# One score product per pair of blocks in stick-breaking attention, and VectorE adding each key's own logarithm

## The reference

```python
log_beta = jax.nn.log_sigmoid(z)
log_stay = jnp.where(mask, log_beta - z, 0.0)          # mask: key_pos < q_pos
log_w = log_beta + lax.cumsum(log_stay, axis=3, reverse=True) - log_stay
w = jnp.where(mask, jnp.exp(log_w), 0.0)
out = einsum('bhqs,bhsd->bhqd', w, v)
```

## Time and profile before

| | us |
|---|---|
| median of 3 runs | 3321.93 (3318.65 to 3331.39) |
| the profiled execution, its own time | 3318.72 |
| its span | 3316.9 |
| PE busy | 3078.7 |
| DVE busy | 2420.3 |
| ACT busy | 1340.9 |
| mean granted TensorE clock | 0.969 |

### The profile page before, as it was taken

One profiled execution on the slowest core, in us unless ns is written; L12 is line 12 of the kernel. 1 busy time (PEld: TensorE's weight loads), 2 busy tenths in 40 slices (PEclk: granted clock), 3 DMA queues, 4 the chain that ended last, 5 costly groups with the idle time before them and its releaser, 6 DMA issues. The chain is left out here.

```text
span 3316.9 us, 45880 instructions
## 1 busy us (share of the span) xinstructions
PE 3078.7 (93%) x16440; PEld 2049.9 (62%) x16440; DVE 2420.3 (73%) x5311; ACT 1340.9 (40%) x3417; POOL 1326.1 (40%) x1040
## 2 busy tenths in 40 slices
PE   7999899889999999988699999998899999999887
PEld 2466488656666666655344565787666666666553
DVE  5874459988889878777721253499888888878777
ACT  3232122786555555400111153226866565555000
POOL 0000000655556767766300000005456656767664
PEclk9999999999999999999899989999999999999999
DMA  8510261989999999999812101518799999999998
GB/s 302 181 51 26 95 228 65 347 291 364 374 371 376 409 409 409 409 408 409 332 57 82 49 22 38 195 67 310 276 359 376 384 353 409 409 409 409 409 409 351
DMA packets 282682, 931.22 MB, mean 281 GB/s; under 512 B 31804, under 2 KB 32460, under 8 KB 281944
## 3 DMA queue, kind: packets, MB, share of 16 engines
q0 software_dynamic: 147840, 536.96, 41.6%
q1 hardware_dynamic: 134616, 391.34, 31.3%
HBM read 921.87 MB, written 6.32 MB: 280 GB/s over the span
## 5 line engine op out<-in xcount | busy, mean ns | idle before, releaser
L753 PE MATMUL psum<-hT,mod 128*128 128x256 f32 x4096 | 969.8, 392 | 64.0 <-ACT big L1211 38.6
L753 PEld LDWEIGHTS psum<-hT,mod 128*128 128x128 f32 x4096 | 782.2, 195 | 189.7 <-issue 86.7
L1221 ACT ACTIVATE levels<-key_numbers,hT 128x128 bf16<-128x128 f32 x1792 | 566.7, 389 | 138.0 <-PE psum L789 137.5
L1871 DVE SCALAR_TENSOR_TENSOR tmp<-w,small,tmp 128x1024 f32<-128x1024 f32 x339 | 435.7, 1285 | 82.3 <-DMA w<-in_peer_v,tmp 37.8
L2046 POOL DMA_INDIRECT w<-in_peer_u,tmp x172 | 236.4, 1374 | 584.2 <-DVEq L1702 447.3
L1851 DVE CUSTOM_DVE_ANT_0 w<-w,hn 128x1024 f32<-128x1024 f32 x342 | 408.7, 1224 | 73.5 <-DMA w<-in_peer_down,tmp 36.2
L2046 POOL DMA_INDIRECT big<-in_peer_down,tmp x86 | 117.5, 1366 | 720.0 <-DVEq L1702 633.7
L763 PE MATMUL psum<-rows,big 128*128 128x512 f32 x768 | 344.2, 592 | 3.3 <-DVE big L1804 3.3
L789 PEld LDWEIGHTS psum<-x,levels 128*128 128x128 bf16 x6144 | 225.7, 101 | 164.8 <-issue 100.9
L1224 ACT ACTIVATE levels<-levels 128x512 bf16<-128x512 bf16 x448 | 282.2, 630 | 14.2
L789 PE MATMUL psum<-x,levels 128*128 128x32 bf16 x6144 | 236.9, 196 | 50.5 <-DVE levels L1792 25.7
(11 more groups left out here) (328 smaller groups left out, 4179.7 us busy)
## 6 DMA issues: line engine op xcount, KB each, us to landing
mod<-in_uT SPq DMA_DIRECT2D x256, 512.0 KB, 6.8
rows<-in_peer_v SPq DMA_DIRECT2D x64, 512.0 KB, 6.8
rows<-in_peer_up SPq DMA_DIRECT2D x64, 512.0 KB, 6.8
w<-in_w_in SPq DMA_DIRECT2D x14, 2048.0 KB, 8.5
srow<-in_peer_v SPq DMA_DIRECT2D x32, 512.0 KB, 6.9
tmp<-in_peer_v SPq DMA_DIRECT2D x32, 512.0 KB, 6.8
srow<-in_peer_up SPq DMA_DIRECT2D x32, 512.0 KB, 6.8
tmp<-in_peer_up SPq DMA_DIRECT2D x32, 512.0 KB, 6.8
```

Source lines behind the costliest of these rows:

```text
L753: last = nc.tensor.matmul(ps[4 + e % 2][:, 0:ND], ub[e % UV][:, k, :], hT[:, k, ND:SEQ], start=k == 0, stop=k == KC - 1)
L1221: last = nc.scalar.activation(hits[n % HITS][:, j * P:(j + 1) * P], keyno, ACT.Abs, bias=nibT[:, n * BATCH + j:n * BATCH + j + 1])
L1871: last = stt(y, row, c8[g % 2][:, b:b + 1], y, ALU.mult, ALU.add)
```

## The change

The first constant matrix becomes the strict triangle, so that a tile's sum holds only later keys. TensorE no longer forms the score a second time: it sums the `stay` tiles alone into bank 6 or 7, the own block first and the later blocks after it. VectorE, after the softplus, makes a second pass over the same PSUM score and `ab` in place: min(z, 0) minus the logarithm, which is the key's own log_beta. For tile m it then waits for `ar_done`, adds the sum in PSUM to that buffer, writes the result to `st1` and raises a new semaphore, `w_added`. ScalarE waits for `w_added` of tile m in place of `ar_done` and raises `st1` in place. The `ab` buffers become four. The mask of the weights on VectorE moves one iteration later (m = n - 3), its loop has one more iteration, and `rstd` and `gated` move two iterations later. TensorE's wait before a sum becomes `w_added`, and the wait for the values of two heads before moves from ScalarE to VectorE.

```diff
--- before.py
+++ after.py
@@ -68,7 +68,7 @@
 
         "c_reset": np.broadcast_to((np.arange(SEQ) % CHUNK != 0).astype(np.float32), (P, SEQ)).copy(),
 
-        "c_sticks": np.stack([-(j >= i).astype(np.float32), -np.ones((P, P), np.float32),
+        "c_sticks": np.stack([-(j > i).astype(np.float32), -np.ones((P, P), np.float32),
                               (j < i).astype(np.float32)], 1).reshape(P, 3 * P),
 
         "c_decay": decay.astype(np.float32),
@@ -334,7 +334,7 @@
         rt = [part(tmp, 2 * n, 2) for n in range(2)]
         sq = part(tmp, 4, 2)
         t3 = part(tmp, 6, 2)
-        ab = [part(tmp, 2 * n, 2) for n in range(LOOK + 1)]
+        ab = [part(tmp, 2 * n, 2) for n in range(LOOK + 2)]
         z_bank = [ps[1], ps[4], ps[5]]
         stay = [part(big, 8 * n, 8).rearrange("p (j n) -> p j n", j=NT) for n in range(2)]
         wide_sq = part(tmp, 10, 2)
@@ -427,6 +427,7 @@
         sp_ready = sem("stays_ready")
         ar_done = sem("stick_logs_summed")
         w_exp = sem("weights_raised")
+        w_added = sem("own_logs_added")
         wt_ready = sem("weights_ready")
         picks_ready = sem("dense_picks_ready")
         picks_turned = sem("dense_picks_turned")
@@ -975,13 +976,12 @@
                 if m >= 0:
                     h, j = m // NT, NT - 1 - m % NT
                     if m >= 2:
-                        pe.wait_ge(w_exp, m - 1)
+                        pe.wait_ge(w_added, m - 1)
                     bank = ps[6 + m % 2]
-                    score(h, j, bank, True, False)
                     pe.wait_ge(sp_ready, m + 1)
-                    for i in range(NT - 1, j - 1, -1):
+                    for i in range(j, NT):
                         last = nc.tensor.matmul(bank[:, (i - j) * P:SEQ - j * P], sticks[:, 0 if i == j else 1, :],
-                                                stay[h % 2][:, i, i * P:SEQ], start=False, stop=i == j)
+                                                stay[h % 2][:, i, i * P:SEQ], start=i == j, stop=i == NT - 1)
                     last.then_inc(ar_done, 1)
                     if h and j == NT - 2:
                         stick_values(h - 1)
@@ -1332,10 +1332,10 @@
             for n in range(STICKS + LOOK):
                 if n < STICKS:
                     wd = SEQ - (NT - 1 - n % NT) * P
-                    z, l = z_bank[n % (LOOK + 1)][:, 0:wd], ab[n % (LOOK + 1)][:, 0:wd]
+                    z, l = z_bank[n % (LOOK + 1)][:, 0:wd], ab[n % (LOOK + 2)][:, 0:wd]
                     act.wait_ge(z_done, STICKS + n + 1)
-                    if n > LOOK:
-                        act.wait_ge(z_used, n - LOOK)
+                    if n >= LOOK + 2:
+                        act.wait_ge(w_added, n - LOOK - 1)
                     step(nc.scalar.activation(l, z, ACT.Abs))
                     step(nc.scalar.activation(l, l, ACT.Exp, scale=-1.0))
                     nc.scalar.activation(l, l, ACT.Ln, bias=1.0).then_inc(ln_ready, 1)
@@ -1349,10 +1349,9 @@
                 m = n - LOOK
                 if m >= 0:
                     h, j = m // NT, NT - 1 - m % NT
-                    act.wait_ge(ar_done, m + 1)
-                    if j == NT - 1:
-                        act.wait_ge(pv_done, 8 + 8 + h - 1)
-                    nc.scalar.activation(st1[h % 2][:, j, j * P:SEQ], ps[6 + m % 2][:, 0:SEQ - j * P], ACT.Exp).then_inc(w_exp, 1)
+                    act.wait_ge(w_added, m + 1)
+                    w = st1[h % 2][:, j, j * P:SEQ]
+                    nc.scalar.activation(w, w, ACT.Exp).then_inc(w_exp, 1)
                     if j == 0 and h >= 1:
                         head_out(h - 1, 64, 512, 8 + 8 + h, stick_sq[(h - 1) % 2], 8 + 4 + h - 2 if h >= 3 else 0)
             head_out(7, 64, 512, 8 + 8 + 8, stick_sq[1], 8 + 4 + 6)
@@ -1974,7 +1973,7 @@
                 nc.vector.tensor_reduce(ss_sticks.rearrange("p (t h) -> p t h", t=NT)[:, :, h],
                                         stick_sq[h % 2].rearrange("p (t n) -> p t n", t=NT), AX_X, ALU.add).then_inc(heads_summed, 1)
 
-            for n in range(STICKS + LOOK):
+            for n in range(STICKS + LOOK + 1):
                 if n in (1, 4, 7, 10):
                     dve.wait_ge(pv_used, 8 + 8)
                     centred(n // 3)
@@ -1982,11 +1981,11 @@
                     seen.next(ss_done)
                     t = n // 3 - 1
                     nc.vector.tensor_reduce(ss[:, 8 * t:8 * t + 8], by_head(wide_sq, 8, 64)[0], AX_X, ALU.add).then_inc(heads_summed, 1)
-                if n == 13:
+                if n == 15:
                     dve.wait_ge(heads_summed, 8 + NT)
                     rstd(8 * NT, 64)
-                if n in (14, 16, 18, 20):
-                    gated(n // 2 - 7)
+                if n in (16, 18, 20, 22):
+                    gated(n // 2 - 8)
                 if n < STICKS:
                     h, j = n // NT, NT - 1 - n % NT
                     wd = SEQ - j * P
@@ -1997,11 +1996,21 @@
                         else:
                             dve.wait_ge(z_done, STICKS + 1)
                     sv_ = stay[h % 2][:, j, j * P:SEQ]
-                    stt(sv_, z_bank[n % (LOOK + 1)][:, 0:wd], 0.0, ab[n % (LOOK + 1)][:, 0:wd], ALU.max, ALU.add).then_inc(z_used, 1)
+                    z, l = z_bank[n % (LOOK + 1)][:, 0:wd], ab[n % (LOOK + 2)][:, 0:wd]
+                    stt(sv_, z, 0.0, l, ALU.max, ALU.add)
+                    stt(l, z, 0.0, l, ALU.min, ALU.subtract).then_inc(z_used, 1)
                     dve.wait_ge(z_used, n + 1)
                     sv_ = stay[h % 2][:, j, j * P:(j + 1) * P]
                     tt(sv_, sv_, sticks[:, 2, :], ALU.mult).then_inc(sp_ready, 1)
                 m = n - LOOK
+                if 0 <= m < STICKS:
+                    h, j = m // NT, NT - 1 - m % NT
+                    wd = SEQ - j * P
+                    dve.wait_ge(ar_done, m + 1)
+                    if j == NT - 1:
+                        dve.wait_ge(pv_done, 8 + 8 + h - 1)
+                    tt(st1[h % 2][:, j, j * P:SEQ], ps[6 + m % 2][:, 0:wd], ab[m % (LOOK + 2)][:, 0:wd], ALU.add).then_inc(w_added, 1)
+                m = n - LOOK - 1
                 if m >= 0:
                     h, j = m // NT, NT - 1 - m % NT
                     dve.wait_ge(w_exp, m + 1)
```

## The result

| | before | changed |
|---|---|---|
| median of the runs, us | 3326.14 (4 runs, 3318.65 to 3331.39) | 3352.25 (4 runs, 3351.72 to 3355.45) |
| ratio of the two | | 1.0086, 95% interval 1.0072 to 1.0101 |
| granted clock, whole span | 0.969 | 0.96 |

The account below looks back on a forecast made before the run. TensorE was taken to pace the steady heads before, and turns between ScalarE and VectorE after. 16 us from the turns and 9 from the clock made 25 us on 3318.72, 3344, median 3347 us; range 3330 to 3369 us.

Parts of the forecast that it names:

- The likeliest case: Whole kernel: turns of ScalarE and VectorE plus a partly halved TensorE clock, 25 us longer, median 3347 us, chance 0.52.
- TensorE sets the pace before, and the stage is the path: Stage before the change: PE paces steady heads at 11.75 us; a microsecond in the 106.4 us stage is one of the kernel.
- The removal saves 2.2 us a head: TensorE's score products: half go, saving 2.2 us a head, so PE needs about 9.5 us a head.
- VectorE's second pass and addition: 3.9 us a head: VectorE's added work in the stage: 3.9 us a head, 31 us in all, making its 52 busy us some 83.
- ScalarE and VectorE take turns, 14.7 us a head: Steady heads: the two engines wait for each other with little overlap, 14.7 us a head against 11.75.
- The root costs 3.05 us: Head 3: the root's two table loads of 1.28 us and the hand-over lie on the path, making it 17.75 us.
- At full clock +16 us: Whole stage at full clock: heads and tail sum to 122.6 us, 16 us more than 106.4.
- The clock adds 9 us: TensorE in the stage: half of the heads at half clock, 2.2 us each, 9 us more.
- the prediction's own signs: Stage profile: large waits for Ln, the addition and PE's `sp_ready` or addition; steady heads 14.5 to 17 us; clock below 0.89.
- Rival 1: Stage: turns of ScalarE and VectorE but TensorE at full clock, +16 us, 3338 us; chance 0.22.
- Rivals 3 and 4: Stage: rival 3, ACT and DVE overlap more, 3322 us, chance 0.09; rival 4, PE remains the bound, 3304 us, chance 0.06.
- Rival 2: Stage: clock stays at 1.2 GHz mostly and PE's 19 us a head set it, +46 us, 3368 us; chance 0.11.

Follow-up runs that it names:

- the fillers: Changed kernel plus three unused 512-column TensorE products a head, after the sums of its first two tiles; stage 141.6 us, ratio 1.0061 to the kernel before.
- the run with ScalarE freed: Changed kernel, but ScalarE raises the sum straight from PSUM, not waiting for VectorE's addition; own logarithm left out of the weights; stage 133.9 us, ratio 1.0027.
- the version with the later exponential: Changed kernel with ScalarE's exponential and the mask of the weights one iteration later, values after the third tile's sums; stage 151.3 us, ratio 1.0056.
- the kernel with the addition first: Changed kernel with VectorE's addition of tile n - 2 ahead of everything else in iteration n; stage 144.0 us, ratio 1.0086 to the kernel before.

## Why the prediction was right

It gave 3347 us and a ratio of about 1.0075; 3352.25 and 1.0086 came. It used the median of three runs, 3321.93, which a fourth moved to 3326.14, so that its 25 us stand against 26.1 between the medians and 28.5 in the stage. The likeliest case is the one that happened. Two errors, in TensorE's need and in the mask of the weights, left the total alone only because the turns were longer; that was luck. Point by point:

- *TensorE sets the pace before, and the stage is the path.* Shown: with half the scores gone and nothing else changed the stage is 10.1 us shorter and the kernel 0.31% faster.
- *The removal saves 2.2 us a head.* Mis-sized: 1.53 us. I halved the time of a group whose members run partly side by side. Scores of neighbouring heads lie on different halves of the partitions (`heads[h % 2]` in `score`), and the trace shows such a pair running side by side: before, the 128-column score of one head and the 384-column score of the head before it take 0.85 us together, from the first product to the next group, and in the run without the second score the 384-column one alone takes 0.83:

```profile
1979.29 0.92 PE L960 MATMUL psum<-big 64*128 64x128 f32 x4
1980.14 1.57 PE L983 MATMUL psum<-big,levels 128*128 128x128 f32 x6
...
2000.29 0.91 PE L960 MATMUL psum<-big 64*128 64x384 f32 x2
...
2001.12 0.49 PE L982 MATMUL psum<-big,levels 128*128 128x128 f32 x2
```

The first two lines are of before, the others of the run. In the same way the 256- and 512-column pair took 1.05 us. The 384- and 128-column scores of one head, which lie on the same half, took 1.06, longer than the 384 alone by the time of the 128. Over the four tiles of a head it is 4.44 us before, of which half is my 2.2, and 2.92 in the run. TensorE's need is 10.2 us a head, not 9.5. At full clock both are shorter than a turn.
- *VectorE's second pass and addition: 3.9 us a head.* Right: 15.4 + 15.6 = 31.0 us for eight heads, 3.88 each.
- *ScalarE and VectorE take turns, 14.7 us a head.* One turn of the changed kernel in its timeline (start us, length us):

```profile
2014.55 0.58 ACT L1339 ACTIVATE tmp<-psum 128x512 f32<-128x512 f32 x1
...
2015.16 0.63 ACT L1340 ACTIVATE tmp<-tmp 128x512 f32<-128x512 f32 x1
2015.82 0.63 ACT L1341 ACTIVATE tmp<-tmp 128x512 f32<-128x512 f32 x1
2016.48 0.69 DVE L2000 SCALAR_TENSOR_TENSOR big<-psum,tmp 128x512 f32<-128x512 f32 x1 [1.98 <-ACT tmp L1341]
2017.09 0.68 DVE L2001 SCALAR_TENSOR_TENSOR tmp<-psum,tmp 128x512 f32<-128x512 f32 x1
2017.80 0.29 DVE L2004 TENSOR_TENSOR big<-big,levels 128x128 f32<-128x128 f32 x1
2018.01 0.42 DVE L2012 TENSOR_TENSOR hT<-psum,tmp 128x256 f32<-128x256 f32 x1
...
2018.17 0.79 PE L961 MATMUL psum<-big 64*128 64x128 f32 x2
...
2018.46 0.42 ACT L1354 ACTIVATE hT<-hT 128x256 f32<-128x256 f32 x1 [2.02 <-DVE hT L2012]
...
2032.88 0.79 PE L961 MATMUL psum<-big 64*128 64x128 f32 x2
```

ScalarE's three steps run to 2016.45; VectorE's first pass starts at 2016.48 and its addition, last of four, at 2018.01; ScalarE's exponential starts at 2018.46 with 2.02 us of idle time ahead of it; VectorE's first pass had 1.98 us of it. From the first product of this head to that of the next it is 14.71 us (2018.17 to 2032.88), at full clock for most of it. It is the shortest of the later heads here; with the fillers four heads took 14.2 to 14.8. That the wait for the addition costs time is shown by the run with ScalarE freed.
- *The root costs 3.05 us.* From the first table load to the exponential it took 3.4 us; its head took 19.3 us against the 17.75 laid out:

```profile
1978.56 1.28 ACT L1025 ACT_TABLE_LOAD   x1
...
1980.44 0.23 ACT L1025 ACTIVATE small<-small 128x32 f32<-128x32 f32 x1 [0.60 <-DVE small L1391]
1980.69 1.28 ACT L1348 ACT_TABLE_LOAD   x1
...
1981.98 0.31 ACT L1354 ACTIVATE hT<-hT 128x128 f32<-128x128 f32 x1
```

- *At full clock +16 us.* The changed kernel with TensorE kept busy, the nearest to that case, is at +15.4 us, with fillers and 35 us at half clock in it (31 before). No run has the turns alone at a clock of 1.00.
- *The clock adds 9 us.* Right in kind, too small: 13.1 us came back with the fillers. The share was near: I had half of the heads at half clock, and 85 of the 154.7 us were. The price was too low: I took 2.2 us for a head at half clock, and the 50 us less of it with the fillers gave back 13.1, by which a head of 15 us at half clock costs some 4 (an estimate). The heads from first read to first read took 11.0, 16.0, 18.1, 19.3, 14.8, 17.7 and 15.6 us against 11.3, 15.6, 14.7, 17.75, 15.3, 15.3 and 14.7 laid out for full clock: 7.8 us over. From there to the last products with the values it was 22.6 us against 18.0, another 4.6. Together 12.4, near the 13.1. The Trainium skill ("TensorE: Matmul & The Clock Gate", "A second HAM failure mode") tells of a kernel in which short and frequent idle times of TensorE between groups of matmuls made its clock go up and down. The trace agrees: it falls nine times in the stage, with no wait of PE for the mask longer than 3.0 us in the waits view.

Turn and clock overlap: 20.8 and 13.1 us one by one, 28.1 together (154.7 to 126.6). By the ratios it is 15 and 4 us one by one, and 22 together. Part of the overlap is that the run with ScalarE freed also lost 26 us of half clock; how far a turn hides a slow matmul was not measured by itself.

What the prediction left out: it took the later mask of the weights as free. In the changed kernel PE waits 16.4 us for it ahead of the values, seven times, and in the version with the later exponential it was the next bound. By the prediction's own signs PE should have waited long for the masked softplus (`sp_ready`) or for the addition; it shows 2.5 us for the first, and 7.2 us of its weight loads for the second. Steady heads were to take 14.5 to 17 us: two of them took 18.1 and 17.7.

Rival 1 fell with the clock of 0.72. Rivals 3 and 4 fell with the turns. Rival 2 had the clock low for most of the stage, and 85 of the 154.7 us were at 1.2 GHz, but TensorE at that clock did not set the pace throughout: it came back in every head.

That the clock falls because TensorE has too little work between its waits is shown by the three fillers a head that held it; which of the gaps decides was not taken apart.

## What to carry to other kernels

Moving work onto an engine that has room by busy time is only half a sum: write down, for each engine, what stands behind each wait, and look for a loop between two engines A and B in which A, after its step n, waits for B's finishing step n - 2, which in B's order stands behind B's step n, which waits for A's step n. Break it by a lag of one iteration more (that alone gained 3.4 us of the 28.5 here), and then look again at everything that hung on the old lag (here the values and the next score behind them). When TensorE is relieved of work and has gaps, count its remaining work at half clock too. And a product that is taken away is worth what it costs beside its neighbours: two that run side by side cost little more than the longer one.

## What the runs showed of the hardware that I had not expected

TensorE with 24 products added was through the same stage sooner than without (141.6 against 154.7 us in the traced executions), with the granted clock at 0.87 in place of 0.72; the kernel's times show only 1.0061 against 1.0073, with overlapping intervals. A wait for TensorE at half clock can take back part of what a better order saves: in the kernel with the addition first, sums of 1280 columns took 4.63 us against 2.42 us at full clock. And two score products on different halves of the partitions ran side by side: 128 and 384 columns in 0.85 us together, where the 384 alone take 0.83 and the same two on one half 1.06.
